# Second block's attention: two pairs of heads per step, weight chunks emptied singly, and the order on ScalarE and VectorE

## The reference

```python
def _sb_attend(qs, qpos, kvs, kpos):
    (q,) = qs
    k, v = kvs
    z = jnp.einsum('bqhd,bkhd->bhqk', q, k).astype(jnp.float32) * (HEAD_DIM ** -0.5)
    mask = kpos[None, :] < qpos[:, None]
    log_keep = jnp.where(mask, jax.nn.log_sigmoid(-z), 0.0)
    later = lax.cumsum(log_keep, axis=3, reverse=True) - log_keep
    a = jnp.where(mask, jnp.exp(jax.nn.log_sigmoid(z) + later), 0.0)
    return jnp.einsum('bhqk,bkhd->bqhd', a.astype(v.dtype), v)

def sb_mixer(h, w_qkv, w_o):
    B, L, _ = h.shape
    qkv = (h @ w_qkv).reshape(B, L, 3, N_HEADS, HEAD_DIM)
    q, k, v = qkv[:, :, 0], qkv[:, :, 1], qkv[:, :, 2]
    o = sweep_queries(_sb_attend, (q,), (k, v))
    return o.reshape(B, L, N_HEADS * HEAD_DIM) @ w_o
```

## Time and profile before

| | us |
|---|---|
| median of 3 runs (1356.3 to 1358.45) | 1356.33 |
| the profiled execution, its own time | 1361.56 |
| its span | 1360.3 |
| PE busy | 1229.8 (90%) |
| DVE busy | 547.4 (40%) |
| ACT busy | 493.2 (36%) |
| POOL busy | 169.3 (12%) |

### The profile page before, as it was taken

How to read it: one execution, slowest core, us unless ns; L and a number is a source line. 1 busy time by engine, 2 the same in 40 slices (tenths; PEclk the granted TensorE clock), 3 DMA queues, 4 the chain that set the end, 5 groups by cost and what they waited for, 6 DMA issues and landing times. The chain is left out here.

```text
span 1360.3 us, 19458 instructions
## 1 busy us (share of the span) xinstructions
PE 1229.8 (90%) x8324; PEld 939.0 (69%) x8324; DVE 547.4 (40%) x638; ACT 493.2 (36%) x604; POOL 169.3 (12%) x173
## 2 busy tenths in 40 slices
PE   7999999799998888888875599999999998999998
PEld 7998888544342323233221489999998998999998
DVE  5664666411111100001002766565453334766643
ACT  6543752221111211111103434434346665444432
POOL 0530000301101011010001530000110000400011
PEclk9999999799999999999997789999998998999999
DMA  9733468399999999999995735554552223465530
GB/s 335 253 127 124 153 244 301 124 396 423 421 422 421 422 422 422 422 421 422 421 415 196 242 102 186 186 167 154 188 174 78 79 93 97 144 219 186 170 115 32
DMA packets 148949, 337.39 MB, mean 248 GB/s; under 512 B 7346, under 2 KB 118107, under 8 KB 124158
## 3 DMA queue, kind: packets, MB, share of 16 engines
q1 hardware_dynamic: 143280, 321.46, 62.7%
q0 software_dynamic: 3216, 9.44, 1.9%
q10 hardware_dynamic: 2366, 5.22, 1.1%
HBM read 329.79 MB, written 6.30 MB: 247 GB/s over the span
## 5 line engine op out<-in xcount | busy, mean ns | idle before, releaser
L1516 DVE TENSOR_TENSOR lo<-raw,hi 128x2048 fp32r<-128x2048 f32 (+1 forms) x112 | 252.0, 2252 | 158.1 <-ACT hi L1084 131.9
L1084 ACT CAST hi<-raw 128x2048 fp32r<-128x2048 f32 (+1 forms) x115 | 213.4, 1857 | 113.5 <-PE PS L433 94.6
L431 PE MATMUL PS<-AH,hi 128*128 128x272 f32 (+1 forms) x832 | 241.0, 290 | 6.9 <-DVE Q L2015 4.3
L433 PE MATMUL PS<-AH,lo 128*128 128x272 f32 (+1 forms) x832 | 239.6, 288 | 0.0
L432 PE MATMUL PS<-AL,hi 128*128 128x272 f32 (+1 forms) x832 | 239.2, 287 | 0.0
L431 PEld LDWEIGHTS PS<-AH,hi 128*128 128x128 f32 x832 | 159.3, 191 | 8.8 <-DVE lo L1516 4.5
L433 PEld LDWEIGHTS PS<-AH,lo 128*128 128x128 f32 x832 | 159.3, 191 | 0.0
L432 PEld LDWEIGHTS PS<-AL,hi 128*128 128x128 f32 x832 | 158.8, 191 | 0.1
L1864 DVE TENSOR_TENSOR HM<-T,PS 64x512 f32<-64x512 f32 x32 | 22.1, 690 | 315.2 <-ACT T L1264 315.2
L1264 ACT ACTIVATE T<-PS 64x512 f32<-64x512 f32 x32 | 18.9, 590 | 238.8 <-PE PS L710 238.8
L432 PE MATMUL PS<-FL,hi 128*128 128x272 f32 (+1 forms) x352 | 100.4, 285 | 0.0
(11 more groups left out here) (401 smaller groups left out, 2184.7 us busy)
## 6 DMA issues: line engine op xcount, KB each, us to landing
raw<-in_w_gate_up_dram SPq DMA_DIRECT2D x48, 1024.0 KB, 26.9
half<-in_w_gate_up_dram SPq DMA_DIRECT2D x45, 1024.0 KB, 27.8
spare<-in_w_gate_up_dram SPq DMA_DIRECT2D x35, 1024.0 KB, 27.0
half<-in_w_down_dram SPq DMA_DIRECT2D x26, 1024.0 KB, 28.1
raw<-in_w_down_dram SPq DMA_DIRECT2D x24, 1024.0 KB, 27.6
raw<-in_ffn_w_gate_dram SPq DMA_DIRECT2D x22, 1024.0 KB, 5.2
raw<-in_ffn_w_up_dram SPq DMA_DIRECT2D x22, 1024.0 KB, 5.2
raw<-in_w_in_dram SPq DMA_DIRECT2D x21, 1024.0 KB, 7.9
```

Source lines behind the costliest of these rows:

```text
L431: pe.matmul(o, w(h, c), xh(k), start=start and c == 0, stop=False)
L433: r = pe.matmul(o, w(l, c), xh(k), start=False, stop=stop and c == len(ks) - 1)
L1084: act.copy(K.view(K.hi[i % HN], 0, [[1, n]]), K.view(K.rbuf[i], 0, [[1, n]])).then_inc(S.hi, 1)
L1516: r = e.tensor_tensor(K.view(K.lo[i % HN], 0, [[1, n]]), K.view(K.rbuf[i], 0, [[1, n]]), K.view(K.hi[i % HN], 0, [[1, n]]).bitcast(F32), A ...
```

## The change

**PE.** Both pairs' `scores` come first, then two units, both `decay`, the third unit, both `out`. The out of a round no longer falls into the next round. `decay` has 4 matmuls in a group: the two of 16 columns against the same weights are one, which reads its 16 columns twice and writes 2 x 16 columns 144 apart. **Chunks.** Each chunk of a Q or K unit and of wo 0 to 3 is taken by its own DVE instruction; chunks go in turn through banks 6 and 7, and PE waits for the chunk two before (`chunk_left`). A new semaphore `qk_pe` counts first chunks. The first V unit goes into banks 0, 1, 2, and the first scores wait for fewer of its chunks. **ACT.** |z| and exp of both pairs, then ln of both, so that one load of each table serves two pairs; the rounding `PH` comes ahead of the unit's split. **DVE.** The first chunk's taking, then `PP` of both pairs, then the second chunk, and `PL`, with the units' `lo` behind it. In wo 3 the additions go ahead of the `lo` of two FFN units, which stand directly ahead of wo 4's additions.

Core of the diff (the signatures that follow from it are left out):

```diff
+def chunk_bank(i, j, m):
+
+    if j == 0:
+        return ((6, 7), (2, 3), (0, 1, 2))[i][m]
+    t = 21 + 2 * i + m if j == 4 else 7 * (j - 1) + 2 * i + m
+    return 6 + t % 2
+
+
+def chunk_left(e, S, i, j, m):
+
+    t = 21 + 2 * i + m if j == 4 else 7 * (j - 1) + 2 * i + m
+    if t < 2:
+        e.wait_ge(S.qk_out, t + 1)
+    elif t - 2 >= 21:
+        e.wait_ge(S.wo_out, t - 2 - 21 + 1)
+    else:
+        jj, c = (t - 2) // 7 + 1, (t - 2) % 7
+        if c < 4:
+            e.wait_ge(S.qk_out, 4 * jj + c + 1)
+        else:
+            e.wait_ge(S.v_out, 3 * jj + c - 4 + 1)
...
-                pe.matmul(o(0, 256), later["trineg"], x(0, 256), start=False, stop=True, skip_group_check=True)
-                pe.matmul(o(112, 144), later["negones"], x(256, 144), start=False, stop=True, skip_group_check=True)
-                pe.matmul(o(256, 160), later["trineg"], x(256, 160), start=False, stop=True, skip_group_check=True)
-                pe.matmul(o(240, 16), later["negones"], x(400, 16), start=False, stop=True, skip_group_check=True)
-                r = pe.matmul(o(384, 16), later["negones"], x(400, 16), start=False, stop=True, skip_group_check=True)
+                pe.matmul(o(0, [1, 256]), trineg, x(0, [1, 256]), start=False, stop=True, skip_group_check=True)
+                pe.matmul(o(256, [1, 160]), trineg, x(256, [1, 160]), start=False, stop=True, skip_group_check=True)
+                pe.matmul(o(112, [1, 144]), negones, x(256, [1, 144]), start=False, stop=True, skip_group_check=True)
+
+                r = pe.matmul(o(240, [144, 2], [1, 16]), negones, x(400, [0, 2], [1, 16]), start=False, stop=True, skip_group_check=True)
...
     for j in range(4):
         g = 2 * j
         scores(g)
-        if j == 3:
-            out(g - 1)
+        scores(g + 1)
         between(0, j)
-        if 0 < j < 3:
-            out(g - 1)
-        scores(g + 1)
         between(1, j)
         decay(g)
+        decay(g + 1)
         between(2, j)
         out(g)
-        decay(g + 1)
+        out(g + 1)
     wo(3)
-    out(7)
     wo(4)
...
     for j in range(4):
         g = 2 * j
-        scores(g)
+        between(0, j, 0)
+        soft(g)
+        soft(g + 1)
+        between(0, j, 1)
+        rest(g)
+        ahead(0, j)
+        rest(g + 1)
+        between(1, j, 0)
+        between(1, j, 1)
+        ahead(1, j)
+        ahead(2, j)
         if j == 3:
-            out(g - 1)
-        between(0, j)
-        rest(g)
-        if 0 < j < 3:
-            out(g - 1)
-        scores(g + 1)
-        between(1, j)
-        rest(g + 1)
-        between(2, j)
+            for m in range(2):
+                between(2, j, m)
         out(g)
-    wo(3)
-    out(7)
-    wo(4)
+        out(g + 1)
+    for m in range(2):
+        wo(3, m)
+    dve_ahead(dve, K, S, K.at["wo", 3], K.NU)
+    dve_ahead(dve, K, S, K.at["wo", 4], K.NU)
```

More of the change, by code:

```diff
@@ L1426, in act_attention, with values @@
     act.copy(K.AMR[:, :], K.AM[:, :]).then_inc(S.act_step, 1)
[L1428 to L1436, removed]
+    def values(j):
         for v in range(3):
-            b = (6, 7)[(v + j) % 2] if j else v % 2
+            b = chunk_bank(2, j, v)
             rows = 128 if v < 2 else 16
@@ L1442, in qkv @@
             else:
-                act.wait_ge(S.unit, n + 1)
+                act.wait_ge(S.unit, K.at["qkv", (2, j)] + 1)
             if j == 0 and v == 0:
@@ L1458, in scores, with log @@
         act.activation(two(E), two(E), ACT.Exp, scale=-1.0).then_inc(own, 1)
-        act.wait_ge(own, 3 + 2 * g + 2)
+    def log(g):
+        E = K.EE[g % 2]
+        act.wait_ge(S.act_own, 3 + 2 * g + 2)
         act.activation(two(E), two(E), ACT.Ln, bias=1.0).then_inc(S.att_ln, 1)
@@ L1472, in out, with ahead @@
         act.copy(view(K.OH2, S_ * g, [[1, S_]]), bank(4 + g % 2, 0, [1, S_])).then_inc(S.o_hi, 1)
[L1474 to L1487, removed]
+    def ahead(i, j):
+        act_ahead(act, K, S, K.at["qkv", (i, j + 1)] if j < 3 else K.at["wo", i])
+    act_ahead(act, K, S, K.at["qkv", (0, 0)])
+    act_ahead(act, K, S, K.at["qkv", (1, 0)])
+    act_rs(act, K, S, K.tc(K.RS, 0, 0), 2)
+    for v, (p0, w) in enumerate(((0, 128), (128, 128), (256, 16))):
+        act_rs(act, K, S, view(K.small, 96 + v, [[1, 1]], rows=w), 3 + v)
+    act_ahead(act, K, S, K.at["qkv", (2, 0)])
+    values(0)
     for j in range(4):
         g = 2 * j
-        scores(g)
-        if j == 3:
-            out(g - 1)
-        between(0, j)
+        soft(g)
+        soft(g + 1)
+        log(g)
+        log(g + 1)
         halve(g)
-        if 0 < j < 3:
-            out(g - 1)
-        scores(g + 1)
-        between(1, j)
+        ahead(0, j)
         halve(g + 1)
+        ahead(1, j)
         decay(g)
-        between(2, j)
+        decay(g + 1)
+        ahead(2, j)
+        if j < 3:
+            values(j + 1)
         out(g)
-        decay(g + 1)
-    wo(3)
-    out(7)
+        out(g + 1)
+    act_ahead(act, K, S, K.at["wo", 3])
     act.wait_ge(S.unit, K.at["qkv", (2, 3)] + 1)
-    wo(4)
+    act_ahead(act, K, S, K.at["wo", 4])
+    for k in range(8):
+        act_chunk(act, K, S, 2, k, par("nf", 8 + k), NMETA)
 def rest_lo(e, K, S, i):
@@ L2006, in dve_attention, with take, soft @@
     dve.memset(view(K.K2, 272, [[384, 8], [1, 112]]), 0.0).then_inc(S.dve_step, 1)
[L2008 removed]
+    def take(i, j, m):
         q0, w = (NMETA, S_) if i == 0 else (0, L)
[L2010 to L2012 removed]
+        dst = view(K.K2, 768 * j + 384 * m, [[1, w]]) if i else view(K.Q2, 512 * j + S_ * m, [[1, w]])
+        if m:
+            dve.wait_ge(S.unit, K.at["qkv", (i, j)] + 1)
+        else:
+            dve.wait_ge(S.qk_pe, 2 * j + i + 1)
         if j == 0:
             dve.wait_ge(S.rs, 2)
[L2015 removed]
+        dve.scalar_tensor_tensor(dst, bank(chunk_bank(i, j, m), 0, [1, w]), 1.0 if i else 0.125, tc(K.RS, 0, q0),
                                  ALU.mult, ALU.mult).then_inc(S.qk_out, 1)
[L2018 to L2031 removed]
+    def soft(g):
         dve.wait_ge(S.att_ln, g + 1)
@@ L2068, in between, with wo @@
-    def between(i, j):
+    def wo(j, m):
+        n, h = K.at["wo", j], tc(K.HH, 2 * j + m, NMETA)
+        if m:
+            dve.wait_ge(S.unit, n + 1)
+        else:
+            dve.wait_ge(S.wo_pe, j + 1)
+        dve.tensor_tensor(h, bank(chunk_bank(j, 4, m), 0, [1, S_]), h, ALU.add).then_inc(S.wo_out, 1)
+    def between(i, j, m):
         if j < 3:
-            qkv(i, j + 1)
+            take(i, j + 1, m)
         else:
-            wo(i)
-    for i in range(3):
-        qkv(i, 0)
+            wo(i, m)
@@ new lines, in ahead @@
+    def ahead(i, j):
+        dve_ahead(dve, K, S, K.at["qkv", (i, j + 1)] if j < 3 else K.at["wo", i], K.NU)
+    dve_ahead(dve, K, S, K.at["qkv", (0, 0)], K.NU)
+    dve_ahead(dve, K, S, K.at["qkv", (1, 0)], K.NU)
+    dve.wait_ge(S.ss, 2)
+    dve_rs(dve, S, own, tc(K.RS, 0, 0), bank(5, 0, [1, L]))
+    dve.wait_ge(S.ss, 3)
+    for v, w in enumerate((128, 128, 16)):
+        dve_rs(dve, S, own, view(K.small, 96 + v, [[1, 1]], rows=w), bank(4, v, [1, 1], rows=w))
+    for i in range(2):
+        for m in range(2):
+            take(i, 0, m)
@@ new lines, in dve_attention @@
+    for m in range(2):
+        wo(3, m)
+    dve_ahead(dve, K, S, K.at["wo", 3], K.NU)
+    dve_ahead(dve, K, S, K.at["wo", 4], K.NU)
+    for m in range(8):
+        if m == 7:
+            dve.wait_ge(S.unit, K.at["wo", 4] + 1)
+        else:
+            dve.wait_ge(S.wo_pe, 4 + m + 1)
+        h = tc(K.HH, m, NMETA)
+        dve.wait_ge(S.wo_out, m + 1)
+        dve.tensor_tensor(h, bank((7, 6, 4, 5)[m % 4], 0, [1, S_]), h, ALU.add).then_inc(S.hu, 1)
+        if m:
+            dve_chunk(dve, K, S, 2, m - 1, par("nf", 8 + m - 1), NMETA)
```

127 lines of the change are left out of this document (41 added, 86 removed).

## The result

The changed kernel takes 1335.41 us (median of 4 runs, 1334.33 to 1336.15) against 1357.39 for the kernel before, run beside it (4 runs, 1356.3 to 1359.08). The ratio is 0.9836, with a 95% interval of 0.9819 to 0.9853: 22 us less, 20 to 25 by the interval. The forecast was 1334.8.

A forecast was written before the change was run, and what follows sets the result against it. PE, busy 90% of the span, was taken as the bound, losing time in the attention to waits and half clock. 23.7 - 2.6 + 2.2 - 1.4 = 21.9, taken as 21.5, gave a median of 1334.8 us, range 1331.5 to 1341.

The forecast's parts named there:

- What can go: PE's losses in the attention: 12.8 us idle, 1.6 of matmul tails, 9.3 from half clock; sum 23.7.
- The round walk: One attention round, engine by engine: slack 2.1 us in rounds 1 and 2, 0.8 in round 0; round 3 waits 0.2.
- the second way: Check from round 2's length: rounds of 29.4 us, attention gain 22.5, less 1.4 is 21.1.
- New wait in wo 4: PE waits 2.4 us in wo 4 behind DVE's last wo 3 addition and two `lo`, replacing the 1.3.
- Decay: 32 decay groups lose one 16-column matmul each, at 0.07 us: 2.2 us gained.
- The bound of 3.8: Upper bound of the decay gain, if the pitch of a 256-column matmul, 0.12 us, goes in each group.
- Half clock behind the new wait: Behind wo 4's new wait, 3.2 to 6.1 us at half clock; 0.7 to 2.2 lost, 1.4 taken.
- The sum: Whole gain: 23.7 - 2.6 + 2.2 - 1.4 = 21.9 us; 21.5 taken.
- Rival 1: Softplus chain later than worked out, second chunks wait: 2 to 4 us a round, 1337 to 1345; chance 0.12.
- Rival 2: ACT's table switch costs more than its row, were it twice 1.3: 8 us, 1342.8; chance 0.03.
- Rival 3: Gain given back behind the attention, FFN waits for a late `raw` buffer: 1340 to 1346; chance 0.04.
- Rival 4: Slower than before: Q's second taking, behind both `PP`, comes late in each round: 1359 to 1363; chance 0.03.

The follow-up runs named there:

- e_ln_apart: Changed kernel, but ACT does exp and ln of one pair, then of the other, with two table loads more in each round: 1342.0 us, ratio 0.9883.
- e_lo_first: Changed kernel, but DVE writes the split's `lo` ahead of the second chunk's taking and of `PL`: 1350.81 us, ratio 0.9944.
- t_tail: Changed kernel with one `lo` between wo 3's additions, the other behind wo 4's last chunk, and wo 4's banks reordered: 1334.03 us, ratio 0.9818.
- e_pair_only: Changed kernel with pairs together and table loads grouped, but old decay, first chunk late, `lo` and `hi` first: 1363.04 us, ratio 1.0039.
- b_again: The kernel before, unchanged, run once more for a second profile: 1358.92 us, ratio 1.0004.
- a_again: The changed kernel, unchanged, run once more: 1336.18 us, ratio 0.9838.
- b_behind: Kernel before, unpaired, with ACT's `PH` ahead of the split and, in rounds 0 to 2, DVE's taking and `PL` ahead of the `lo`: 1352.46 us, ratio 0.9951.
- b_merge: The kernel before with only the changed kernel's decay, 4 matmuls in a group: 1355.68 us, ratio 0.9974.
- e_first_late: Changed kernel, but DVE takes a unit's first chunk behind both `PP`, with the second: 1343.01 us, ratio 0.9891.

## Why the prediction was right, point by point

That the time is only 0.6 us off is partly luck, a balance of errors. By the steps of the prediction:

- **What can go, 23.7.** Shown: every wait named has gone, and rounds 0 to 2 run with PE busy throughout at clock 1.00. The size of one term was that of one execution: half clock was worth 9.3 in the first profile and 7.9 in the second. With 7.9 the sum is 22.3.
- **The round walk.** Right in its numbers: first chunk 6.2 us into the round (6.0 forecast), `PP` twice from 7.4 us on in round 1 (7.5 forecast) and from 8.6 in round 0, second chunk out by 10.9 in round 0, which leaves 1.1 us (0.8 forecast), and e_ln_apart and e_lo_first both give 2.4 for rounds 1 and 2 (2.1 forecast). In round 3 the wait of 0.2 at wo 1's second chunk did not come. The rounds take 28.9 us, 0.5 less than the 29.4 of the second way; 8 x 0.04 = 0.3 of that is the decay.
- **New wait in wo 4, 2.4.** It is 2.3, in the place and by the queue named (4.48 us of `lo` behind wo 3's last addition). t_tail takes that queue away, and the wait goes.
- **Decay, 2.2.** Mis-sized: 3.5 by the trace. I took the distance of the two 16-column matmuls' starts. The record shows starts, and the merged group closes up by 0.11, more than that one distance. The bound of 3.8 held it.
- **Half clock behind the new wait, -1.4.** Wrong: it cost 0 in both profiles of the changed kernel. I let the waits of 2.6 and 2.3 speak for this one. The same wait at the same place was followed by full clock in the changed kernel and by half clock in e_pair_only (below). Even there it cost next to nothing: from wo 4's fifth chunk to the sum of squares PE takes 16.11 us in e_pair_only and 16.00 in the changed kernel. In the changed kernel PE's starts ahead of 1137.42, 1138.29 and 1139.05 lie 0.3 to 0.4 us further apart than its work takes; in e_pair_only those gaps are gone, and with them nearly the whole loss of 1.4 us (12 matmuls). The forecast had let only 0.9 of the loss disappear in this way.
- **The sum.** With what was measured: 12.8 idle + 1.6 tails + 7.9 - 2.5 (the new wait and its tail) + 3.5 = 23.3, which answers to the 23.1 that the traces of b_again and the changed kernel give for the attention, and to the 23.4 between the medians of a_again and of before beside it. The first result, 22.0, has an interval of 20 to 25 and does not tell 21.5 from 23.3. So my two errors on the changed kernel both made the gain too small, by 2.7 us in all, and the term taken from a single profile made it too large, by 1.4. The rest is the 0.4 by which I went below my own sum of 21.9, and 0.1 in the new waits.

**The rivals.** Rival 1 (second chunks late) did not occur, but it was near: 2.6 us on the same chain bring it about in round 0 and round 3 and cost 6.6 us (e_ln_apart). Rival 2 (a dearer switch) is excluded by the 1.29 to 1.30 from load to next function in all rows shown, and by e_ln_apart, where eight switches more came out under the forecast, not over.
By the Trainium skill, "ScalarE: Activation LUTs", section "What ACT_TABLE_LOAD costs", there would be a drain of 1.38 us on top of each; the trace does not agree.
Rival 3 (given back behind) did not occur: 200.7 us before as after. Rival 4 is the mechanism of e_pair_only and e_lo_first: Q's second taking some 4 us late is what a careless order gives, and without the first chunk's own taking and with the old decay it ends at 1363.04, as that rival had it (1359 to 1363). The change as made does not meet its condition.

**Of my theory's rivals** none stands: pairing alone is slower, the order alone gives 6.5 of the 22, the decay 3.3. The rest, some 12 us, came only with all parts together: pairing, the order in all four rounds, and chunks emptied singly. In b_behind round 3's waits for a `lo` and for an output's rest, 6.9 us, remain, and in the changed kernel they are absent; that pairing is what removes them is argued, since b_behind kept DVE's order of round 3. No run has the kernel before with its chunks emptied singly, or with a new order in round 3, and still one pair at a time. So what pairing itself is worth is open.

## What to carry to other kernels

Grouping two items so that they share a setup (here a table load) lengthens the chain that the other engines' small jobs stand behind; it pays only if those jobs (emptying a bank that PE wants next) are cut smaller and put ahead of or between the long ones, and the large optional work goes last. Walk one period from its start, engine by engine, and write down the slack at each bank that comes free: here 1.1 to 2.4 us of slack decided over 15 us, since a wait of 2 to 5 us often, though not always, cost another 1.7 to 3 us in a lowered clock. And take terms that come from the clock from two profiles of the same program, not from one.

## What the hardware showed that I had not expected

**A wait and the clock behind it.** The same 2.3 us wait of PE ahead of wo 4's fifth chunk, with the same work on all engines behind it, once behind it in e_pair_only (columns as in rows 1):

```profile
1159.50:1163.30 3.80, 3.80 (x22) 3.80 (x21) 3.80 (x11) 2.13 (x5) 3.35 (x5) 0.55 1.10 357
```

and in the changed kernel:

```profile
1133.13:1136.93 3.80, 3.80 (x34) 3.80 (x33) 3.80 (x11) 2.14 (x5) 3.36 (x5) 1.00 1.09 357
```

The first has 22 matmuls in 3.8 us, the second 34. Seven other profiles with this wait (the repetition, both decay kernels, first chunk late, ln apart, `lo` first, `hi` first) show no half clock behind it either. The wait of 2.6 us at the start of wo 0 in round 3 goes the same way: in both profiles of the kernel before it was followed by half clock (19 matmuls in 3.8 us), in b_merge by none:

```profile
1122.19:1125.99 3.80, 3.80 (x31) 3.48 (x33) 3.08 (x4) 0.98 (x2) 0.00 (x0) 1.00 0.14 24
```

In the kernel before a wait of 1.2 us, and in b_merge one of 1.6, was followed by 3.5 us at half clock. Two waits of 1.8 in e_lo_first, one of 1.5 in e_ln_apart and one of 2.1 in e_first_late were followed by none, and the remaining waits of 2.0 to 5.0 by 3 to 6 us. So the length of the wait alone does not decide. What else does is open; it was not tried.
The Trainium skill, "TensorE: Matmul & The Clock Gate", section "Loop structure matters more than you think", has it that a DVE copy out of PSUM between outputs does not break the clock's warmth, where the next output's matmuls follow immediately. In e_first_late nothing is late but such copies, PE waits 2.0 us for one, and 3.4 us at clock 0.51 follow: the sentence does not carry over to a copy that PE has to wait for. The Trainium skill, "TensorE: Matmul & The Clock Gate", section "What's actually happening" of Part 1, says that the number of matmuls at the low clock at a kernel's start differs from run to run of one kernel. For the start no run here looks at it; behind a wait the two profiles of the kernel before differ in the same way (3.5 and 6.1 us behind the same wait).

**A small matmul isn't free.** One matmul of 32 columns in the place of two of 16 makes a group 0.11 us shorter, nearly what one of 256 columns takes from start to start in the wo units (0.12, 1132.55 to 1132.67 in the changed kernel).

**POOL beside a long DVE instruction.** POOL's additions and squares of 128x256 take 0.6 to 0.8 us beside DVE's short instructions, and 2.5 to 2.7 where a `lo` of 2.3 us runs on DVE: two such in the changed kernel (1140.41 and 1144.80, with `lo` at 1140.12 and 1144.60), three in t_tail. Each time the added time is close to the length of the `lo`, and both in the changed kernel end 0.5 to 0.6 us behind the `lo`'s end, about what such an instruction takes by itself. What holds POOL up, no run here tells; that PE's wait follows POOL's end in t_tail, and that POOL's chain there takes 1.8 us longer, speaks for a real delay and not for a drawing.
